# Attention results by feature instead of by token, with the softmax's reciprocal sums folded into the transposes

## What is computed

```python
# block 1, forgetting attention (8 heads of 64)
s = einsum('bhqd,bhkd->bhqk', qb, k) * scale + cb[..., :, None] - cum[..., None, :]
p = softmax(where(causal, s, NEG_INF));  o = einsum('bhqk,bhkd->bhqd', p, v)
out_a = from_heads(o) @ w_fox_up
# block 1, NSA (8 query heads, 2 key groups): compressed, selected and window branches
o = g[..., 0:1] * o_cmp + g[..., 1:2] * o_slc + g[..., 2:3] * o_win
out_b = from_heads(o) @ w_nsa_up
x = x + (sigmoid(g_a) * out_a + sigmoid(g_b) * out_b) @ w_out
x = x + hierarchical_moe(rms_norm(x))
# layers 1 and 2: HGRN2 beside sliding-window attention (16 heads, window 128, sinks)
q_h, f_h, i_h, z_h, q_a, k_a, v_a, z_a = split(rms_norm(x) @ w_in)
o_a = sliding_window_attention(rotary(q_a), rotary(k_a), v_a, sinks) * silu(z_a)
o_h = rms_norm(hgrn2(q_h, f_h, i_h)) * silu(z_h)
x = x + rms_norm(concat([o_h, o_a]) @ w_out)
```

## Time and profile before

| what | before |
|---|---|
| median of 3 runs | 1220.43 us (1215.7 to 1221.11) |
| the profiled execution, own time | 1216.97 us |
| its span | 1214.8 us |
| PE busy | 1079.9 us (89%), 6089 matmul instructions |
| DVE busy | 838.6 us (69%) |
| ACT busy | 671.2 us (55%) |
| POOL busy | 71.1 us (6%) |
| mean granted clock of TensorE | 0.942 of full speed |
| chain that ended last | PE 59%, DVE 21%, ACT 9%, DMA 5%, issue 4% |

### The profile page before, as it was taken

The page is one execution under the profiler, slowest core; times in us unless marked ns, Lnnn a source line. Parts: engine busy times, 40 slices in busy tenths (PEclk is TensorE's granted clock), DMA queues, the critical chain, the costliest instruction groups (busy, mean ns, idle before and its releaser), DMA issues.

```text
span 1214.8 us, 16346 instructions
## 1 busy us (share of the span) xinstructions
PE 1079.9 (89%) x6089; PEld 930.8 (77%) x6089; DVE 838.6 (69%) x1516; ACT 671.2 (55%) x1324; POOL 71.1 (6%) x46
## 2 busy tenths in 40 slices
PE   5789798769599999999988899999887889999887
PEld 4668686668588887787877888888766888888766
DVE  5566553456559999999975866686567766587654
ACT  5345374524378988788854487523335378633233
POOL 0100200000010101003000000100101000010100
PEclk9989798879689999999999999999898999999889
DMA  8522124304149999999964322332243322332220
GB/s 333 173 104 105 57 83 162 115 36 174 36 162 398 348 379 365 351 381 369 388 233 161 134 105 104 139 139 105 88 156 130 144 108 105 143 135 105 88 86 35
DMA packets 30034, 211.44 MB, mean 174 GB/s; under 512 B 3328, under 2 KB 3712, under 8 KB 4992
## 3 DMA queue, kind: packets, MB, share of 16 engines
q1 hardware_dynamic: 28368, 205.01, 45.1%
q10 hardware_dynamic: 1584, 5.34, 1.2%
HBM read 209.28 MB, written 1.05 MB: 173 GB/s over the span
## 4 chain that ended last, share of the span: by engine, by line
PE 59%; DVE 21%; ACT 9%; DMA 5%; issue 4%; POOL 2%; SPq 0%; DVEq 0%; POOLq 0%
PE ps L484 15%; PE ps L486 14%; PE ps L485 14%; DVE w_lo L383 9%; DMA ring<-in_panels 5%; PE ps L489 4%; PE ps L925 3%; ACT s_buf L1737 3%; PE ps L633 2%; ACT L1737 2%; POOL stat L395 2%; DVE gates L383 1%; PE ps L691 1%; DVE scr L383 1%; DVE op_lo L383 1%
## 5 line engine op out<-in xcount | busy, mean ns | idle before, releaser
L383 DVE TENSOR_TENSOR w_lo<-ring,w_hi 128x512 fp32r<-128x512 f32 x760 | 488.4, 700 | 201.0 <-ACT w_hi L1690 200.2
L1690 ACT ACTIVATE w_hi<-ring 128x512 fp32r<-128x512 f32 x760 | 424.8, 620 | 249.5 <-PE ps L486 216.2
L484 PE MATMUL ps<-w_hi,op_hi 128*128 128x512 f32 (+2 forms) x928 | 370.5, 399 | 21.6 <-DVE w_lo L383 13.4
L485 PE MATMUL ps<-w_lo,op_hi 128*128 128x512 f32 (+2 forms) x928 | 361.5, 390 | 0.0
L486 PE MATMUL ps<-w_hi,op_lo 128*128 128x512 f32 (+2 forms) x928 | 361.5, 390 | 0.0
L484 PEld LDWEIGHTS ps<-w_hi,op_hi 128*128 128x128 f32 x928 | 177.9, 192 | 63.3 <-DVE w_lo L383 22.2
L486 PEld LDWEIGHTS ps<-w_hi,op_lo 128*128 128x128 f32 x928 | 177.3, 191 | 36.4
L485 PEld LDWEIGHTS ps<-w_lo,op_hi 128*128 128x128 f32 x928 | 177.9, 192 | 32.0
L484 PE MATMUL ps<-op_hi,w_hi 128*128 128x256 f32 x448 | 134.5, 300 | 8.2 <-DVE op_lo L383 8.2
L485 PE MATMUL ps<-op_lo,w_hi 128*128 128x256 f32 x448 | 130.5, 291 | 0.0
L486 PE MATMUL ps<-op_hi,w_lo 128*128 128x256 f32 x448 | 130.2, 291 | 0.0
(11 more groups left out here) (226 smaller groups left out, 1059.1 us busy)
## 6 DMA issues: line engine op xcount, KB each, us to landing
ring<-in_panels SPq DMA_DIRECT2D x194, 1024.0 KB, 6.4
cst<-in_c ACTq DMA_DIRECT2D x1, 1219.0 KB, 5.3
buf_a<-in_pre ACTq DMA_DIRECT2D x2, 512.0 KB, 6.2
keys<-in_post ACTq DMA_DIRECT2D x2, 512.0 KB, 3.6
out<-x_tok SPq DMA_DIRECT2D x2, 512.0 KB, 2.6
cst<-in_c ACTq DMA_DIRECT2D x1, 960.0 KB, 7.0
x_tok<-in_x SPq DMA_DIRECT2D x1, 512.0 KB, 4.7
x_tok<-in_x ACTq DMA_DIRECT2D x1, 512.0 KB, 4.9
```

The lines of the kernel that those rows point to most:

```text
L383: return V.tensor_tensor(o, a, b, op)
L484: T.matmul(o, l[0], r[0], start=start, stop=False)
L485: T.matmul(o, l[0], r[1], start=False, stop=False)
L1690: return A.activation(o, a, ACT.Copy, scale=scale)
```

## The change

**Reciprocal sums.** `turn_out`'s reciprocal becomes `weigh`: DVE waits for the exponentials (`score_p`), forms the reciprocal of the sums (for NSA times the branch's gate) and writes four 128x128 diagonal matrices: identity times a column of reciprocals. `turn` on PE is then no transpose but a float32 matmul of the exponentials with such a diagonal, and waits for DVE (`weighed`) instead of ACT. **Values** are stationary (64 columns for each head, in the two column halves of the array), the turned probabilities stream with 256 and 128 columns: the result is by feature. `up_turns` and `att_turn` with their transposes go; what is left of them is splitting (`values_out` on ACT for forgetting attention, `up_split`, `att_split`). **z_a** is made by feature, in takes 10 to 17 of a layer, and multiplied in by DVE in `values_out`; POOL's `att_gate` goes; the takes of q and f move to 18 to 33. On DVE `weigh` and `scores_out` now stand in `ahead(t)`, before the take's result is read out. In block 1 `fox_norms` moves from take 12 to 9, NSA's sides from 25 to 26 and its jobs to odd takes, compression's steps by up to one take, and its raw weights one half panel forward.

```diff
-L_QA, L_KV, L_QF, L_ZA, L_IH, L_ZH, L_ATT, L_HG = 0, 8, 10, 26, 34, 42, 50, 58
+L_QA, L_KV, L_ZA, L_QF, L_IH, L_ZH, L_ATT, L_HG = 0, 8, 10, 18, 34, 42, 50, 58
...
+            if n == 8 and h == 1:
+                out += [(2 * PN_CMP + i, 0, None) for i in range(2)]
             if n == 9 and h == 0:
-                out += [(2 * PN_CMP + i, 0, None) for i in range(2)]
-            if n == 9 and h == 1:
                 out += [(2 * PN_CMP + 2 + i, 0, None) for i in range(2)]
...
     for take, scores, turn, values in rows:
-        for name, job in (("values", values), ("turn", turn), ("scores", scores)):
+        for name, job in (("weigh", turn), ("values", values), ("turn", turn), ("scores", scores)):
             if job is not None:
                 table.setdefault(take, []).append((name, job))
-                table.setdefault(take + 1, []).append((name + "_out", job))
+        for name, job in (("turn_out", turn), ("scores_out", scores), ("values_out", values)):
+            if job is not None:
+                table.setdefault(take + 1, []).append((name, job))
...
-    table = {12: [("fox_norms", 0)], 13: [("fox_q", 0)], 14: [("fox_k", 0)], 24: [("nsa_norms", 0)],
-             25: [("nsa_sides", 0)]}
+    table = {9: [("fox_norms", 0)], 13: [("fox_q", 0)], 14: [("fox_k", 0)], 24: [("nsa_norms", 0)],
+             26: [("nsa_sides", 0)]}
     at_ticks(table, [(15, 0, None, None), (17, 1, 0, None), (19, 2, 1, 0), (21, 3, 2, 1), (23, None, 3, 2),
-                     (25, None, None, 3), (26, 4, None, None), (28, 5, 4, None), (30, 6, 5, 4), (32, 7, 6, 5),
-                     (34, 8, 7, 6), (36, 9, 8, 7), (38, 10, 9, 8), (40, 11, 10, 9), (41, None, 11, 10),
+                     (25, None, None, 3), (27, 4, None, None), (29, 5, 4, None), (31, 6, 5, 4), (33, 7, 6, 5),
+                     (35, 8, 7, 6), (37, 9, 8, 7), (39, 10, 9, 8), (40, 11, 10, 9), (41, None, 11, 10),
                      (42, None, None, 11)])
-    for take, step in ((27, 0), (28, 1), (29, 2), (31, 3), (34, 4), (35, 5), (36, 6), (37, 7), (38, 8), (39, 9),
-                       (40, 10), (41, 11), (43, 12)):
+    for take, step in ((28, 0), (29, 1), (30, 2), (31, 3), (34, 4), (35, 5), (36, 6), (37, 7), (38, 8), (39, 9),
+                       (40, 10), (41, 11), (42, 12)):
...
             def turn(job):
-                pe.wait_ge(score_p, job + 1)
+                pe.wait_ge(weighed, job + 1)
                 pe.wait_ge(turn_out, job)
                 for e in range(2):
                     for i, c in enumerate((S, 0, P)):
-                        m = turn128(ps[:, 4 + e, i * P:(i + 1) * P], s_of(job)[:, e * 384 + c:e * 384 + c + P])
+                        m = T.matmul(ps[:, 4 + e, i * P:(i + 1) * P], s_of(job)[:, e * 384 + c:e * 384 + c + P],
+                                     weight_of(job, 1 if i else 0, e), start=True, stop=True)
...
-                for e in range(2):
-                    cc = c + e * HD
-                    T.matmul(o[:, 0, e, :], pt[:, e * 384:e * 384 + P], v3[:, 0, cc:cc + HD], start=True, stop=True)
-                    for kt in range(2):
-                        m = T.matmul(o[:, 1, e, :], pt[:, e * 384 + (kt + 1) * P:e * 384 + (kt + 2) * P], v3[:, kt, cc:cc + HD],
+                for kt in range(2):
+                    for e in range(2):
+                        half, cc = slice(e * HD, (e + 1) * HD), c + e * HD
+                        pt = pt_of(job)[:, e * 384:(e + 1) * 384]
+                        m = T.matmul(ps[half, 6, kt * P:S], v3[:, kt, cc:cc + HD], pt[:, kt * S:S + kt * P],
                                      start=kt == 0, stop=kt == 1)
...
-            def up_turns(which):
...
-            def att_turn(l):
...
-            def turn_out_(job):
+            def weigh(job):
                 _, _, sm, ex, rec = job_stats(job)
                 dve.wait_ge(score_p, job + 1)
-                dve.wait_ge(value_out, job - 1)
                 if job >= L1_JOBS:
+                    dve.wait_ge(pre_x, 4 * ((job - L1_JOBS) // SWA_PAIRS + 1))
                     dv(tt(sm, sm, ex, ALU.add))
                     settle()
-                V.reciprocal(rec, sm).then_inc(row_sum, 1)
+                dv(V.reciprocal(rec, sm))
+                settle()
+                if FOX_JOBS <= job < L1_JOBS:
...
+                    dv(tt(rec3, rec3, ng[:, :, branch, 2 * r:2 * r + 2], ALU.mult))
+                    settle()
+                dve.wait_ge(turn_mm, job)
+                for a in range(TT):
+                    for e in range(2):
+                        m = ts(weight_of(job, a, e), ident[:, :], rec[:, 2 * a + e:2 * a + e + 1], None, ALU.mult)
+                m.then_inc(weighed, 1)
...
+                tt(zb3[:, :, c:c + P], o, za[:, r * S:(r + 1) * S].rearrange("p (a t) -> p a t", a=TT),
+                   ALU.mult).then_inc(value_out, 1)
...
+            def ahead(t):
+                feed(2 * t + AHEAD)
+                for name, arg in beside.get(t, ()):
+                    if name in ("weigh", "scores_out"):
+                        table[name](arg)
...
                 for t in range(t0, t0 + L2_TAKES - 3):
-                    feed(2 * t + AHEAD)
+                    ahead(t)
```

More of the change, by code:

```diff
@@ L169, in beside_layer @@
             table.setdefault(b + L_IH + 2 * lv + j, []).append(("level", (l, lv, j)))
[L170 removed]
+    table.setdefault(b + 49, []).extend([("cross", (l, 0)), ("cross", (l, 1))])
     table.setdefault(b + 50, []).append(("hgrn_values", (l, 0)))
@@ L967, in hg_turn @@
                 pe.wait_ge(hg_out, 4 * l + 4)
+                for a in range(TT):
+                    pe.wait_ge(out_free[a], OUT_L1 + OUT_L2 * (l + 1))
                 for b in range(4):
@@ L991, in pe_program @@
                 which, i = divmod(t - T_UP, 4)
-                if i == 0:
-                    up_turns(which)
                 up_take(t, which, i)
@@ L1602, in dve_program @@
                 which, i = divmod(t - T_UP, 4)
-                if i == 0:
-                    for n in range(2):
-                        dve.wait_ge(up_hi, 2 * which + n + 1)
-                        o = operand(1024 * which + n * 512, 512)
-                        tt(o[1], ps[:, n, :], o[0].bitcast(F32), ALU.subtract).then_inc(up_lo, 1)
-                feed(2 * t + AHEAD)
+                ahead(t)
                 b = i % 2
@@ L1746, in turn_out_, with values_out, up_split, att_split @@
                 copy(pt_of(job).rearrange("p (e c) -> p e c", e=2), ps[:, 4:6, 0:384]).then_inc(turn_out, 1)
+            def values_out(job):
+                if job < FOX_JOBS:
+                    act.wait_ge(value_mm, job + 1)
+                    copy(fox_rows(job)[0], ps[:, 6, 0:S]).then_inc(value_hi, 1)
+            def up_split(_):
+                act.wait_ge(cmp_v, 8)
+                for r in range(PAIRS):
+                    act.wait_ge(value_out, 9 + r)
+                    copy(tm(op_hi[:, 1024 + r * S:1024 + (r + 1) * S]),
+                         z3[:, :, ZNQ + r * P:ZNQ + (r + 1) * P]).then_inc(up_hi, 1)
+            def att_split(arg):
+                l, a = arg
+                act.wait_ge(value_out, L1_JOBS + SWA_PAIRS * (l + 1))
+                for h in range(2):
+                    c = ZQA + h * 512
+                    copy(att_hi[:, a * D + h * 512:a * D + (h + 1) * 512], zb3[:, a, c:c + 512]).then_inc(split_hi, 1)
             def compress(step):
@@ L1921, in act_program @@
                 which, i = divmod(t - T_UP, 4)
-                if i == 0:
-                    for n in range(2):
-                        act.wait_ge(up_T, 2 * which + n + 1)
-                        c = 1024 * which + n * 512
-                        copy(op_hi[:, c:c + 512], ps[:, n, :]).then_inc(up_hi, 1)
                 feed(2 * t + AHEAD)
```

239 lines of the change are left out of this document (127 added, 112 removed).

## The result

| | before | after |
|---|---|---|
| median | 1220.77 us (4 runs) | 1321.74 us (4 runs, 1321.24 to 1325.21) |
| ratio after to before | | 1.0843, 95% interval 1.0809 to 1.0878 |
| span of the profiled execution | 1214.8 us | 1323.4 us |
| mean granted clock | 0.942 | 0.917 |
| PE busy | 1079.9 us | 1120.9 us |

The change costs 101 us, not the 67 that were forecast; 1321.7 lies above the range, which ended at 1316. The direction and the new wait came as predicted, two terms of the sum did not.

The account below looks back on a forecast made before the run. In the layers, ACT's chain in a closed ring was taken to set the time. Profiled 1217 + 63 (layers) + 2 (z_a) - 5 (att_turn) - 7 (block 1) + 14 (clock) = 1284, median 1287 us; range 1245 to 1316.

Parts of the forecast that it names:

- The new wait: Each layer job: `turn` waits for DVE's diagonals, behind two low parts; 3.4 us more, bounds 2.8 and 3.8.
- The dearer turn: `turn` as twelve float32 matmul instructions takes 1.35 us instead of six transposes' 0.80: 0.55 us more a job.
- The rounds without the clock: Seven rounds of a layer, turn to turn, before any clock loss: 94.8 us against 67.4.
- The clock: Longer waits in the layers' 16 jobs drop PE's clock about every other time, 1.7 us each: +14 us, bounds 0 and 27.
- rival 3: Every wait in the layers drops the clock and block 1 gives nothing back: 1307 us, median 1310; chance 15%.
- Block 1: Forgetting attention +8.5, shorter wait at the forget gates -4.4, NSA -10.5: -7 us in all, bounds -22 and +8.
- NSA from its first turn to the second up projection: Block 1 stretch of 124.9 us, written out job by job as 105, plus about 8 for slow clock.
- the forget gates': In block 1, norms three takes earlier shorten the 4.9 us wait behind the forget gates and its slow clock: -4.4 us.
- Rival 1: Diagonals covered: ready with the exponentials, or no two splits before them; 1203 us, about 1206 on the median; chance 7%.
- the ring: Layer job's closed chain, `turn`, `scores`, a whole take, ACT's work, next `turn`: 9.47 us, predicted to become 13.4.
- Rival 2: The clock holds in the layers' longer waits, the ring is paid without drops: 1270 us, median 1273; chance 25%.

Follow-up runs that it names:

- e1: Changed kernel, but in the layers DVE does `weigh` before the two low parts of the same take; 1281.66 us, ratio 1.0506.
- e10: Changed kernel; layers' odd take reordered: ACT high parts, copy, exponentials, then take's result; DVE mask, maxima, low parts, job's result, `weigh`, take's result; 1223.03 us.
- e4: Changed kernel, with sixteen unread 128x128 float32 matmuls on PE before each layer `turn` waits for the diagonals; 1290.84 us, ratio 1.0594.
- e2: Changed kernel, but `turn` waits for ACT's exponentials and multiplies by the identity, leaving out the reciprocal sums; 1217.61 us, ratio 0.9981.
- e9: Changed kernel, but at takes 41 and 42 DVE does `values_out` of jobs 9 and 10 before `weigh`; 1314.90 us, ratio 1.0778.
- e11: e10 plus, in block 1, `weigh` of jobs 0 to 9 before the low parts and `values_out` of jobs 9 and 10 before `weigh`; 1201.42 us.
- e5: Changed kernel with `fox_norms` moved back from take 9 to take 12; 1322.74 us, ratio 1.0855.

## Why the prediction was wrong

**The new wait: right.** All its parts and their order stand in the chain. The four diagonals took 0.89 instead of 1.1 us, so the wait was a little cheaper than priced: 3.1 us, not 3.4.

**The dearer turn: a little too small.** At the high level the distance from `turn` to `scores` is 1.53 us (712.64 to 714.17 in e1), not 1.35. Before, `turn` began at 712.79 and `scores` here:

```profile
713.60 0.92 PE L633 MATMUL ps<-keys,zin 64*128 64x256 f32 x8
```

That is 0.81 us, so the change costs 0.72 us more, not 0.55. The rate of 0.11 us was taken from another row; here twelve instructions last 1.60 us, of which the last one's own is 0.28, so one comes every 0.12 us. Why the two rates differ, no run shows. `values` gave 0.5 us back where PE was the bound (e10).

**The rounds without the clock: right in size.** Computed 94.8 us for seven, measured 93.6 (e4). The layers' cost without the clock came to 60.1 us, against 63 + 2 - 5 = 60. That this sum fits so closely is in part luck. The rounds of both layers came to +52.8 us (54.8 booked, and part of z_a's 2), and up to the first turn +6.1 (6.8 booked). Behind the last turn, where 1.1 - 5 = -3.9 was booked, the two layers took 168.5 and 165.4 us in e4 against 166.9 and 165.7 before, +1.2.

**The clock: the first step that failed.** "So such a wait drops the clock about every other time": one like wait had dropped it and one had not, and I took the mean of the two. All sixteen waits of the layers are longer than both of these (4.0 us and more), and no round kept the clock. That was rival 3's half on the clock, which had 15%. The layers lost 33 us to it (e4), not the 14 booked, and more than the upper bound of 27: a drop cost 1.9 to 2.1 us a round, not 1.7. The argument against the mean stood in the text, that the new waits are longer than the one that dropped it. The Trainium skill ("TensorE: Matmul & The Clock Gate", What's actually happening), quoted there, pointed the same way, and the trace agrees with it: 0.81 to 0.87 in all fourteen rounds. The chance was set too low.

**Block 1: the second.** Booked at -7 (its parts add up to 8.5 - 4.4 - 10.5 = -6.4), bounds -22 and +8; measured +10.9, outside the bounds. Forgetting attention came nearly as computed: 12.56 us a round, against 12.5. What failed is NSA from its first turn to the second up projection. It took 124.9 us before; the sum had 105, and 8 more for the slow clock. The chain of the changed kernel has these ends:

```profile
160.13 1.60 PE ps L668 x12
...
284.31 0.36 PE ps L504
```

That is 124.2 us, 11 more than booked. The gain was there: without the waits for the diagonals block 1 falls by 13.9 us (e2). Two orders take it away. In jobs 9 to 11 the reading of one job's result stands on DVE behind the `weigh` of the next, which was in no part of the sum: 7.9 us of the kernel's time (e9). And low parts stand before `weigh`, with the slow clock behind the waits: about 14 us, by difference only (e11 against e10, 21.6 us of medians less e9's 7.9). The sum had the two splits as a term (1.9 us a round), so how much of these 14 it missed stays open. The other 4.4 us are the forget gates': the shorter wait behind them was bought with a longer one in front (e5), so the gain booked for it was none.

**The stage that nobody touched.** Router and experts were booked at 0 and came 4.4 us longer. None of the variants edits them, and they took 323.1 us in e11's trace, 324.6 in e4's, 328.9 in the change's, 330.5 in e2's; the kernel before and its two variants lie at 323.7 to 324.5. So a span of 7 us between kernels with the same code there covers the +4.4; whether a part of it is an effect of the change stays open.

**Not tried alone.** att_turn, z_a, and the moves of NSA's jobs and of compression in block 1. For att_turn and z_a the layers' sum in e4 holds only together with the rounds, as said above.

**Rivals.** Rival 1 asked whether the diagonals are covered. They weren't. The nearest run to its case is e2, where `turn` waits for none: 1217.6, not the 1206 of that rival. Its second condition, that two splits do not stand before the diagonals, was not enough: e1 has it in the layers, waits of 2.3 us stay, and the time is 1281.7. That e11 comes to 1201 is no proof of it, since there the odd take is out of the ring too. Rival 2, with the clock held in the layers, is e4: 1290.8 against 1273, and the 18 us between them are block 1. Rival 3 is what came, 12 us above its figure: its block 1 stood at +3, its layers at +87 (measured 93.3), and the stage in between at nothing.

Together: the clock +19, block 1 +18, the stage in between +4, make the 41 us between 67 and 108.6 on the profiled spans; against the medians' 101 they are 7 to 8 us too many, by the choice of the two profiled executions.

## What to carry to other kernels

When a producer moves to another engine, write down what stands in front of it there, and what that in turn waits for: two fifths of this loss (e1) went away with two unrelated low parts that stood there and waited for ACT. A wait that recurs on the tensor engine costs itself and then the slow work behind it; if the trace has one drop and one hold at some length and the new waits are longer and stand in every round, give a drop in each of them the larger chance, and don't forecast from a mean. This is a bet, not a rule: in e1 a wait of 2.79 us kept the clock and several of 2.30 lost it. Before a chain is called bound by an engine, see whether it runs through a piece of work that only the order puts into it: here the ring held a whole take, and taking it out (with the splits beside the exponentials, not before or behind them) gave back 99 of the 101 us that the change had cost.

## What the runs showed of the hardware

- A repeated wait of 4.0 us left PE at the low clock level behind it in every round seen in the layers (`turn` 2.30 to 2.93 us instead of 1.60, granted clock 0.81 to 0.87); one of 2.3 to 2.8 us did so in some rounds and not in others (e1); one of 1.0 to 1.5 us (e2) or of 0.26 to 0.75 (e4) in none. A drop cost 1.6 us with the same work (11.50 and 13.10 us), 1.9 and 2.1 on average over seven rounds.
- Matmuls whose result nobody reads, put into a wait, made the changed kernel 31 us faster (e4).
- Twelve instructions of a float32 matmul took 1.53 us to the next start at the high level and six transposes 0.75 to 0.81; at the low level `turn` took 2.93 and 1.54.
- The untouched stage of router and experts was between 323.1 and 330.5 us long in the traces of thirteen kernels.
